# Mixer rounds 2, 3, 21, 22 and 23 reordered, and the memory panels of the stick-breaking half rounded one step later

## The chip, the cores and the metric

The kernel runs as one program on one core of a Trainium2 chip. The metric is the device time of one execution in microseconds (us). The kernel before took 2021.67 us (median of three runs, 2021.38 to 2026.02).

## The reference, cut to what matters

A sequence of 256 tokens of width 1024 (float32) goes through two blocks.

- First block, two layers. Each: `ada = silu(c) @ w_ada[l] + b_ada[l]` (1024 x 6144) gives shifts, scales and gates; `h = rms_norm(x) * (1 + sc) + sh`; `h @ w_in[l]` (1024 x 4888) gives the queries, keys and values of two mixers and the branch gates. The first mixer (NSA, 8 heads of width 64) attends three times: to 15 compressed blocks, to selected blocks (here all four, so causal attention) and to a window (causal too). The second mixer (MoBA) is causal attention over 8 heads. Their outputs go through `w_up_nsa`, `w_up_moba`, the gates and `w_out`, then a SwiGLU follows.
- Second block, two layers, each with two half SwiGLUs, a mixer and a cross attention to a memory of 256 tokens. The mixer of its layer 0 has a differential half and a stick-breaking half. The stick-breaking half is, for each of 8 heads, with z the scaled scores:

```
log_beta = log_sigmoid(z)
log_keep = where(strict, log_sigmoid(-z), 0)
later = cumsum(log_keep, reversed) - log_keep
w = where(strict, exp(log_beta + later), 0);  out = w @ v
```

The cross attention's keys and values are `rms_norm(mem) @ xm_w_kv` (1024 x 1024, in four panels of 512 rows by 512 columns).

## The kernel before, in words

**Weights.** All weights stream through `ring`, three slots of 1 MB, in the order of one list of panels (`weight_panels`). A panel holds 4 x 128 rows by 512 columns. SyncE issues a panel's DMA when the panel three places before it is released. Each dense product is made in three matmuls of rounded parts: high weight part x high and low activation part, and low weight part x high activation part. So each dense panel is split: ScalarE (ACT) copies it to the rounded high part ("hi", 2048 elements a partition, L753), VectorE (DVE) subtracts to get the low part ("lo", L2362) and releases the slot. The parts lie in two buffers, so a high part waits until TensorE (PE) has used the panel two before. `splits.until(key, ahead)` in an engine's program makes all parts in the list that are still to be made up to that panel and `ahead` more dense ones. Panels of `w_ada` are not multiplied on PE: VectorE multiplies and adds them itself, four passes over 512 columns for each half ("ada half", L2366 and L2371), and releases them. In the first block's mixers the list alternates: win4.0, win4.1, ada a, win5.0, ada b, win5.1, ada c, gbr0.0, and so on to gbr3.1, ada, nsa0 (`w_up_nsa`), ada, nsa1, moba0, moba1.

**Mixer rounds.** Each first-block layer has one loop of 27 rounds over 24 heads (8 selected, 8 window, 8 MoBA). Every engine has a loop of its own over i. PE in round i: scores of head i (L1758), transposes of the probabilities of head i-2 (L1770), weighted values of head i-3 (L1783), and two of the steps of the dense work beside it (a step is one chunk of 128 rows, 6 or 12 matmuls, L1550), which write banks from the pair `FILL`, freed by ScalarE's evacuation (two copies to `tok` and, for some, two squares to `sq`). VectorE in round i: the mask pass of head i (`masked`, L2590), which gives the row maxima `nmax`; then two steps of its side list (`more`), which hold the low parts. ScalarE: the copy of the transposed head i-2 (`turned_copy`), two exponentials of head i (`exps`, which wait for `nmax`), then its two steps of `more`, which hold high parts and evacuations. Engines run in order; between them there are only semaphores.

In round 3 VectorE adds mask and scale to the compressed scores (`cmp_s`, tile `feat`), takes the maximum and subtracts it ("cmp shifted"), and ScalarE exponentiates them ("cmp probs"). PE transposes the NSA output `y` at the end of round 21 (`tr y`, banks 6 and 7); ScalarE rounds it to the high part of `y_mix` (`y_copies`) in round 22, VectorE makes its low part (`y_lo`, which frees the two banks) in round 23. In round 23 PE opens banks 6 and 7 for the last four MoBA heads ahead of the weighted values of head 20. In round 24 PE starts `w_up_nsa`, which needs the low part of nsa0, `y_lo`, and banks 4 and 5, which VectorE frees in `moba_out(0)` in round 23.

**Stick half.** In `diff_mixer` the second loop has 11 rounds over 8 heads. PE in round i: z of head i, `later` of head i-1 (L2153 to L2155, waits for "keep"), weighted values of head i-3, two steps of the memory's keys and values (`kv_steps`, panels xkv0.0, xkv0.1, xkv1.0, xkv1.1; L1550). ScalarE: softplus of head i (Abs, Exp, Ln on `sq`), the exponential of head i-2, then two steps of `kv_beside(0)`, with high parts and evacuations (`kv_out`). VectorE: for head i three passes to "keep" (`rot`), one pass for head i-1 (`log weight`), one for head i-2 (`weight`), two steps of its own `kv_beside` (low parts, sums of squares, key normalization), and the entries of the dictionary `between`, which finish the differential half.

Of the kernel before, what the change touches and what calls it, by code (L numbers as in the profile page):

```python
# [112 lines left out]
class Tally:  # L113
# [19 lines left out]
    def at(self, key):  # L133
        if self.known is None:
            return self.sems("dve_step"), 1
        name, n = self.known[0][key]
        return self.sems(name), n
# [114 lines left out]
def build(nc, w, known):  # L252
# [7 lines left out]
    with ExitStack() as ctx:  # L260
# [490 lines left out]
        def _(act):  # L751
# [134 lines left out]
            def kv_beside(l):  # L886

                for g in range(2):
                    for n in range(2):
                        for k in range(4):  # L890
                            if k == 3:
                                if n:
                                    squared = kv_out(l, g)
                                splits.until(((("xkv", l), g, n)), 1 if g and n else 2)
                            if g == 1 and n == 0 and k == 2:
                                rsqrts(normed)
                            yield
                    if g == 0:
                        normed = squared

            def rsqrts(squared):

# [122 lines left out]
            def first_block(l):  # L1025
                norm(("mix", l), ("win", l), lambda c: adac[:, l, c:c + 1], ORDER[0])
                pieces = {0: [(0, 8, HD, "nq")], 1: [(C_KS - 512, 2, HD, "ks")],
                          2: [(0, 2, HD, "kw")], 3: [(0, 8, HD, "mq")]}

                def win_out(i):  # L1030
                    squared = []
                    for t in range(TT):
                        squared += evacuate((("win", l, i), t),
                                 [(0, EDGES[i + 1] - EDGES[i], tok_in[:, t, EDGES[i]:EDGES[i + 1]])],
                                 pieces[i])
                    return squared

                for i in ORDER[0:3]:
                    splits.until((("win", l), i, 1), 2)
                    rsqrts(win_out(i))  # L1040

                for kv in range(2):
                    job = ("hid", l, kv)
                    b = psum[:, tally.bank(job), 0:32].rearrange("p (g n) -> p g n", g=2)
                    act.wait_ge(*at(("full", job)))
                    act.wait_ge(*at(("pads", l)))
                    done = [("hid act", l, kv), ("free", job)]
                    if kv == 0:
                        run(hid_k[:, :, 0:NCMP], b[:, :, 0:NCMP], ACT.Gelu_apprx_tanh,
                            "act_hidden", *done)  # L1050
                    else:
                        for g in range(2):
                            run(hid_v[:, g, :, 0:NCMP], b[:, g, 0:NCMP].unsqueeze(1).broadcast_to(
                                [P, 4, NCMP]), ACT.Gelu_apprx_tanh, "act_hidden",
                                *(done if g else ()))
                splits.until((("win", l), 3, 0), 2)
                for j in range(2):
                    copies(("tr nq", l, j), nq_t[:, 2 * j:2 * j + 2, :])
                act.wait_ge(*at(("tok", (("win", l, 2), 1))))
                run(gates[:], tok_in[:, :, C_G:C_QB], ACT.Sigmoid, "act_gates", ("nsa gates", l))  # L1060
                act.preload_act_table_set(EXP_LN)
                copies_apart(("tr ks", l), gk_t[:, 0:1])
                squared = win_out(3)
                job = ("kc", l)
                k = n_sq[0]
                n_sq[0] += 1
                act.wait_ge(*at(("full", job)))
                act.wait_ge(*at(("sq read", k - 2)))
                b = psum[0:16, tally.bank(job), 0:2 * HD]
                run(kcn[:], b.rearrange("p (g d) -> p g d", g=2), ACT.Copy, "act_tok", ("tok", job))  # L1070
                run(sq[0:16, k % 2, 0:2 * HD], b, ACT.Square, "act_sq", ("sq", k), ("free", job))
                rsqrts(squared)
                act.wait_ge(*at(("sq read", k)))
                rsqrt(rs[0:16, k % 4, 0:2], ss[0:16, k % 4, 0:2], HD, "act_rs", ("rs", k))

                heads = mixer_heads(l)
                base = n_att[0]
                n_att[0] += HEADS
                more = beside(l)
                for i in range(HEADS + LAG + 1):  # L1080
                    if i == 15:
                        copies_apart(("tr mk", l, 0), mk_t[0])
                    if LAG <= i < HEADS + LAG:
                        m = i - LAG
                        turned_copy(heads[m], base + m)
                    if i < HEADS:
                        exps(heads[i], base + i,
                             heads[i]["n"] + (8 if heads[i]["st"][0] == "win" else 0))
                    if i == 0:
                        splits.until((("win", l), 3, 1), 2)  # L1090
                    if i == 1:
                        job = ("tr kc", l)
                        act.wait_ge(*at(("full", job)))
                        act.wait_ge(*at(("kc zeros", l)))
                        for g in range(2):
                            r = slice(HD * g, HD * g + HD)
                            run(kc_t[r, 16 * g:16 * g + 16], psum[r, tally.bank(job), 0:16], ACT.Copy,
                                "act_copied", *([("copied", job), ("free", job)] if g else []))
                        copies_apart(("tr kw", l), gk_t[:, 1:2])
                    if i == 3:  # L1100
                        act.wait_ge(*at(("cmp shifted", l)))
                        run(cmp_s, cmp_s, ACT.Exp, "act_step", ("cmp probs", l))
                    if i == 9:
                        for j in range(2):
                            copies(("tr mq", l, j), mq_t[:, 2 * j:2 * j + 2, :])
                    if i == 16:
                        act.wait_ge(*at(("full", ("scores", ("win", l), 7))))
                        copies_apart(("tr mk", l, 1), mk_t[1])
                    if i == 22:
                        for j in range(2):  # L1110
                            y_copies(("tr y", l, 0, j), 2 * j, y_mix)
                    if i == 25:
                        y_copies(("tr y", l, 1, 0), 4, y_mix)
                    for _ in range(UNITS):
                        next(more, None)
                    if i == 5:
                        copies(("cmp turn", l), cmp_pt)
                for _ in more:
                    pass
                y_copies(("tr y", l, 1, 1), 6, y_mix)  # L1120
                for g in range(2):
                    for i in range(2):
                        if g == 0:
                            splits.until((("w_up_moba", l), i, 0), 2)
                        c = 4 * g + 2 * i
                        act.wait_ge(*at(("merged sum", l, c)))
                        run(h[:, 0, c:c + 2, :], rot[:, i, :].rearrange("p (c s) -> p c s", s=S),
                            ACT.Copy, "act_hi", ("merged hi", l, c))
                splits.until((("wout", l), 1, 1))
# [1230 lines left out]
        def _(dve):  # L2360
# [360 lines left out]
            def first_block(l):  # L2721
# [160 lines left out]
                for i in range(HEADS + LAG + 1):  # L2882
                    if i < HEADS:
                        masked(heads[i]["st"], heads[i]["i"], con("causal"), HD ** -0.5)
                    if i - 1 in ADA_AT and pending:
                        ada_take(*pending.pop(0))
                    if i == 4:
                        splits.until(("ada", *ADA_GROUPS[st][0], 1))
                    if i == 5:
                        compressed_weights()  # L2890
                        ks_mk = [head_sums(8, HD) for t in range(TT)]
                        for _ in range(UNITS):
                            next(more, None)
                    if i == 22:
                        splits.until(("ada", *ADA_GROUPS[st][5], 0))
                    if i == 23:
                        for j in range(2):
                            y_lo(("tr y", l, 0, j), 2 * j, y_mix)
                    if i and i != 4:
                        for _ in range(UNITS):  # L2900
                            next(more, None)
                    if i == 0:
# [175 lines left out]
            def diff_mixer():  # L3078
# [103 lines left out]
                def difference_normed(t):  # L3182
# [10 lines left out]
                lb = shifted  # L3193
                more = kv_beside(0)
                between = {0: difference, 1: difference_sums,
                           3: lambda: difference_normed(0), 4: lambda: difference_normed(1)}
                for i in range(11):
                    if i < 8:
                        job = ("z", i)
# [397 lines left out]
```

## Time and profile before

| | |
|---|---|
| median of three runs | 2021.67 us |
| the profiled execution | 2020.08 us |
| its span | 2018.2 us |
| PE busy | 1971.9 us (98%) |
| VectorE busy | 1465.6 us (73%) |
| ScalarE busy | 1099.4 us (54%) |
| mean granted clock of TensorE | 0.997 |

The profile is of one execution; its span leaves out what lies before the first and after the last instruction. In a timeline row the first number is the start, the second how long the row's instructions took together, and the bracket, where there is one, is how long the engine was idle just before and what released it. Rounds are found by counting heads: the mixer loop of layer 0 runs from 87 to 220 us, that of layer 1 from 517 to 650 us, the stick half from 1162 to 1212 us.

### The profile page before, as it was taken

The page shows a single profiled execution, that of the slowest core. Times are in us where ns is not written, and L with a number is a line of the kernel's source. Part 1 is how long each engine was busy: PE and PEld are TensorE (multiplying, and loading weights), DVE is VectorE, ACT ScalarE, POOL GpSimd, SP SyncE. Part 2 cuts the span into 40 slices and gives each one's busy share as a digit, 9 for nine tenths or more (in the row PEclk, how much of TensorE's full clock was granted, in tenths as well). Part 3 has the DMA queues.
Part 4 walks back from the last instruction along what each step waited for, and adds up shares of the span by engine and source line. Part 5 has one row for each costly group of instructions (what it writes and reads, how often), then busy time and mean ns, then how long its engine had stood idle before and what let it go on. Part 6 is the DMA issues. An engine that isn't in the chain of part 4 may idle for free. (4 is left out here: it accounts for less than half of the span.)

```text
span 2018.2 us, 32166 instructions
## 1 busy us (share of the span) xinstructions
PE 1971.9 (98%) x12902; PEld 1772.6 (88%) x12902; DVE 1465.6 (73%) x2326; ACT 1099.4 (54%) x1744; POOL 30.1 (1%) x66
## 2 busy tenths in 40 slices
PE   8999999999999999999999989999999999999999
PEld 5889988898799988898898879888898899899888
DVE  7888788858797786567757586777667748767774
ACT  4655554534665455455546666655455537855552
POOL 1001000000010000000000000000000000000000
PEclk9999999999999999999999999999999999999999
DMA  9566568765566485556556334455555554235554
GB/s 352 164 208 210 188 206 265 264 204 169 169 215 218 150 271 182 184 178 188 188 169 206 127 104 147 147 188 186 175 183 188 188 178 128 94 126 168 188 178 136
DMA packets 266213, 372.24 MB, mean 184 GB/s; under 512 B 8400, under 2 KB 160336, under 8 KB 266064
## 3 DMA queue, kind: packets, MB, share of 16 engines
q1 hardware_dynamic: 264736, 368.91, 56.0%
q8 instruction: 103, 1.69, 0.3%
q10 hardware_dynamic: 1328, 1.26, 0.2%
q14 instruction: 46, 0.38, 0.1%
HBM read 369.09 MB, written 1.05 MB: 183 GB/s over the span
## 5 line engine op out<-in xcount | busy, mean ns | idle before, releaser
L2362 DVE TENSOR_TENSOR parts<-ring,parts 128x2048 fp32r<-128x2048 f32 (+2 forms) x304 | 675.9, 2223 | 398.8 <-ACT parts L753 398.4
L753 ACT ACTIVATE parts<-ring 128x2048 fp32r<-128x2048 f32 (+2 forms) x304 | 565.4, 1860 | 541.9 <-PE psum L1558 320.4
L1558 PE MATMUL psum<-h,parts 128*128 128x512 f32 x1920 | 679.0, 397 | 0.0
L1556 PE MATMUL psum<-h,parts 128*128 128x256 f32 x1920 | 541.8, 282 | 0.0
L1558 PEld LDWEIGHTS psum<-h,parts 128*128 128x128 f32 x1920 | 362.1, 189 | 87.5
L1556 PEld LDWEIGHTS psum<-h,parts 128*128 128x128 f32 x1920 | 360.6, 188 | 1.7 <-DVE parts L2362 1.4
L1550 PE MATMUL psum<-h,parts 128*128 128x256 f32 (+1 forms) x2088 | 257.3, 282 | 4.8 <-DVE h L2371 2.2
L1550 PEld LDWEIGHTS psum<-h,parts 128*128 128x128 f32 (+1 forms) x2088 | 245.8, 188 | 7.8 <-issue 3.3
L1550 PE MATMUL psum<-parts,h 128*128 128x512 f32 (+1 forms) x864 | 208.0, 392 | 8.1 <-ACT sq L753 3.6
L1550 PEld LDWEIGHTS psum<-parts,h 128*128 128x128 f32 x864 | 156.7, 191 | 41.2 <-issue 6.1
L1550 PE MATMUL psum<-hid_hl,parts 128*128 128x256 f32 x1584 | 190.9, 283 | 0.9 <-DVE parts L2362 0.9
L1550 PEld LDWEIGHTS psum<-hid_hl,parts 128*128 128x128 f32 x1584 | 189.5, 189 | 2.6 <-DVE parts L2362 2.5
L1558 PE MATMUL psum<-hid_hl,parts 128*128 128x512 f32 x528 | 185.6, 394 | 0.0
L1556 PE MATMUL psum<-hid_hl,parts 128*128 128x256 f32 x528 | 149.6, 283 | 0.2 <-DVE parts L2362 0.2
L753 ACT ACTIVATE tok<-psum 128x512 f32<-128x512 f32 (+3 forms) x156 | 90.0, 577 | 74.5 <-PE psum L1558 61.3
L1558 PEld LDWEIGHTS psum<-hid_hl,parts 128*128 128x128 f32 x528 | 99.3, 188 | 22.5
L1556 PEld LDWEIGHTS psum<-hid_hl,parts 128*128 128x128 f32 x528 | 99.4, 188 | 0.5 <-DVE parts L2362 0.5
L753 ACT ACTIVATE scores_area<-scores_area,nmax 128x256 f32<-128x256 f32 (+1 forms) x160 | 72.2, 455 | 50.6 <-DVE nmax L2590 50.3
L2362 DVE TENSOR_TENSOR tok<-psum,tok 128x512 f32<-128x512 f32 x120 | 82.1, 684 | 1.9 <-ACT tok L753 1.6
L753 ACT ACTIVATE scores_area<-psum 128x384 f32<-128x384 f32 (+1 forms) x80 | 39.7, 496 | 52.0 <-PE psum L1770 51.7
L2371 DVE SCALAR_TENSOR_TENSOR feat<-ring,scol,feat 128x512 f32<-128x512 f32 x84 | 63.4, 755 | 3.8
L2590 DVE CUSTOM_DVE_ANT_0 scores_area<-psum,const,sums 128x128 f32<-128x128 f32 (+1 forms) x96 | 37.3, 427 | 37.2 <-PE psum L1758 32.3
(271 smaller groups left out, 2128.5 us busy)
## 6 DMA issues: line engine op xcount, KB each, us to landing
ring<-in_w_ffn_in SPq DMA_DIRECT2D x88, 512.0 KB, 4.9
ring<-in_ffn_w_gate SPq DMA_DIRECT2D x88, 512.0 KB, 4.0
ring<-in_ffn_w_up SPq DMA_DIRECT2D x88, 512.0 KB, 5.0
ring<-in_w_ada SPq DMA_DIRECT2D x43, 1024.0 KB, 5.4
ring<-in_w_in SPq DMA_DIRECT2D x36, 1024.0 KB, 5.1
ring<-in_ffn_w_down SPq DMA_DIRECT2D x32, 1024.0 KB, 5.1
ring<-in_w_ffn_out SPq DMA_DIRECT2D x16, 1024.0 KB, 5.0
ring<-in_ffn_w_down SPq DMA_DIRECT2D x16, 768.0 KB, 4.4
```

Source lines behind the costliest of these rows:

```text
L753: act.activation(out, in_, func, **kw).then_inc(*sig(name, *keys))
L1550: mm = pe.matmul(out, left, right, start=start and n == 0, stop=stop and n == 2, skip_group_check=True)
L1556: pe.matmul(bank[:, 0:S], wt_hl[1], act[:, 0, :], start=start, stop=False, skip_group_check=True)
L1558: return pe.matmul(bank.rearrange("p (a s) -> p a s", a=2), wt_hl[0], act, start=False, stop=stop, skip_group_check=True)
L2362: dve.tensor_tensor(out, a, b, op).then_inc(*sig(name, *keys))
L2371: dve.scalar_tensor_tensor(out=out, in0=a, scalar=s, in1=b, op0=op0, op1=op1, **kw).then_inc(*sig(name, *keys))
L2590: dve.tensor_tensor_reduce(to, of, add, times, 3.0e38, ALU.add, ALU.min, nmax[:, n % 3, t:t + 1]).then_inc(*sig("dve_nmax", *keys))
```

## The change

ScalarE, mixer loop: the exponential of the compressed scores in round 3 goes behind the two steps of that round; the two `y_copies` go from round 22 to round 21. VectorE, mixer loop: round 2 makes only the ada half and leaves its two steps to round 3, behind the mask pass of head 3 and ahead of the compressed scores; the two `y_lo` go from round 23 to round 22, ahead of the ada half; the two steps of round 22 (low part of nsa0) go to round 23, behind the mask pass of head 23. Stick half, ScalarE: each high part that stood at the end of an odd round (k == 3) is made one step later, in the next even round, behind its softplus and exponential. Stick half, VectorE: `difference_normed(1)` goes from round 4 to round 5. No operation is added or taken out, and PE's program is unchanged.

```diff
@@ kv_beside(l), ScalarE
                         for k in range(4):
-                            if k == 3:
-                                if n:
-                                    squared = kv_out(l, g)
-                                splits.until(((("xkv", l), g, n)), 1 if g and n else 2)
+                            if k == 0 and (g or n):
+                                splits.until((("xkv", l), *((g, 0) if n else (0, 1))), 2)
+                            if n and k == 3:
+                                squared = kv_out(l, g)
                             if g == 1 and n == 0 and k == 2:
                                 rsqrts(normed)
                             yield
                     if g == 0:
                         normed = squared
+                splits.until((("xkv", l), 1, 1), 1)
@@ first_block(l), ScalarE
-                    if i == 3:
-                        act.wait_ge(*at(("cmp shifted", l)))
-                        run(cmp_s, cmp_s, ACT.Exp, "act_step", ("cmp probs", l))
...
-                    if i == 22:
+                    if i == 21:
                         for j in range(2):
                             y_copies(("tr y", l, 0, j), 2 * j, y_mix)
...
                     for _ in range(UNITS):
                         next(more, None)
+                    if i == 3:
+                        act.wait_ge(*at(("cmp shifted", l)))
+                        run(cmp_s, cmp_s, ACT.Exp, "act_step", ("cmp probs", l))
@@ first_block(l), VectorE
+                    if i == 2:
+                        splits.until(("ada", *ADA_GROUPS[st][0], 0))
+                    if i == 3:
+                        for _ in range(UNITS):
+                            next(more, None)
                     if i == 4:
                         splits.until(("ada", *ADA_GROUPS[st][0], 1))
...
                     if i == 22:
+                        for j in range(2):
+                            y_lo(("tr y", l, 0, j), 2 * j, y_mix)
                         splits.until(("ada", *ADA_GROUPS[st][5], 0))
                     if i == 23:
-                        for j in range(2):
-                            y_lo(("tr y", l, 0, j), 2 * j, y_mix)
-                    if i and i != 4:
+                        for _ in range(UNITS):
+                            next(more, None)
+                    if i and i not in (2, 4, 22):
                         for _ in range(UNITS):
                             next(more, None)
@@ diff_mixer(), VectorE
                 between = {0: difference, 1: difference_sums,
-                           3: lambda: difference_normed(0), 4: lambda: difference_normed(1)}
+                           3: lambda: difference_normed(0), 5: lambda: difference_normed(1)}
```

## Rows read from the trace of the kernel before

**Rows 1.** Page, part 1: busy time of each engine.
```profile
PE 1971.9 (98%) x12902; PEld 1772.6 (88%) x12902; DVE 1465.6 (73%) x2326; ACT 1099.4 (54%) x1744; POOL 30.1 (1%) x66
```
**Rows 2.** Waits of PE, whole span: us in total, times, longest.
```profile
...
PE psum L1783 <- DVE y_mix L2362: 4.1, 2, 2.1
PE psum L2153 <- DVE rot L2362: 4.0, 2, 2.6
PE psum L1550 <- ACT sq L753: 3.6, 2, 1.8
...
```
**Rows 3.** Timeline of PE, layer 0, rounds 3 and 4.
```profile
...
102.17 3.01 PE L1550 MATMUL psum<-parts,h 128*128 128x512 f32 x12
...
108.57 4.59 PE L1550 MATMUL psum<-parts,h 128*128 128x512 f32 x12 [1.79 <-ACT sq L753]
...
```
**Rows 4.** Windows: PE, PEld, DVE, ACT, POOL busy (x), PEclk, DMA share, GB/s.
```profile
...
109.00:112.60 3.60, 3.60 (x11) 2.79 (x10) 0.82 (x2) 2.51 (x6) 0.00 (x0) 0.53 0.45 114
...
203.00:207.00 4.00, 1.93 (x17) 1.77 (x16) 3.23 (x11) 0.99 (x4) 0.00 (x0) 1.00 1.03 392
...
```
**Rows 5.** Timeline of ACT, layer 0, round 3.
```profile
...
104.66 0.40 ACT L753 ACTIVATE scores_area<-scores_area,nmax 128x128 f32<-128x128 f32 x1 [2.38 <-DVE nmax L2590]
...
106.11 0.42 ACT L753 ACTIVATE feat<-feat 128x256 f32<-128x256 f32 x1 [0.46 <-DVE feat L2362]
106.43 0.58 ACT L753 ACTIVATE tok<-psum 128x512 f32<-128x512 f32 x1
...
```
**Rows 6.** Timeline of DVE, layer 0, rounds 2 and 5.
```profile
...
101.79 2.29 DVE L2362 TENSOR_TENSOR parts<-ring,parts 128x2048 fp32r<-128x2048 f32 x1
...
113.85 0.29 DVE L2590 CUSTOM_DVE_ANT_0 scores_area<-psum,const 128x128 f32<-128x128 f32 x1 [3.99 <-PE psum L1758]
...
```
**Rows 7.** Timeline of PE, layer 0, rounds 23 and 24.
```profile
...
205.33 0.85 PE L1783 MATMUL psum<-tok,scores_area 128*128 128x64 f32 x6 [2.07 <-DVE y_mix L2362]
...
208.41 3.08 PE L1550 MATMUL psum<-y_mix,parts 128*128 128x256 f32 x24
...
```
**Rows 8.** Timeline of ACT, layer 0, rounds 21, 22 and 26.
```profile
...
198.15 1.92 ACT L753 ACTIVATE parts<-ring 128x2048 fp32r<-128x2048 f32 x1 [1.05 <-DMA ring<-in_w_up_nsa]
...
201.21 1.06 ACT L753 ACTIVATE y_mix<-psum 128x512 fp32r<-128x512 f32 x2
...
217.69 1.92 ACT L753 ACTIVATE parts<-ring 128x2048 fp32r<-128x2048 f32 x1
...
```
**Rows 9.** Timeline of DVE, layer 0, round 23.
```profile
...
203.90 1.28 DVE L2362 TENSOR_TENSOR y_mix<-psum,y_mix 128x512 fp32r<-128x512 f32 x2
...
205.88 0.76 DVE L2362 TENSOR_TENSOR y<-psum,wt 128x256 f32<-128x256 f32 x2
...
```
**Rows 10.** Timeline of SyncE's queue: issues of the panels moba0 and moba1.
```profile
...
203.07 7.17 SPq L674 DMA_DIRECT2D ring<-in_w_up_moba  x2
...
```
**Rows 11.** Timeline of PE, stick half, round 6.
```profile
...
1196.30 0.67 PE L2153 MATMUL psum<-rot,const 128*128 128x256 f32 x2 [2.55 <-DVE rot L2362]
...
1197.84 4.60 PE L1550 MATMUL psum<-parts,mem_hl 128*128 128x512 f32 x12
...
```
**Rows 12.** Timeline of ACT, stick half: high part, then softplus of head 4.
```profile
...
1183.21 1.93 ACT L753 ACTIVATE parts<-ring 128x2048 fp32r<-128x2048 f32 x1
1185.01 0.50 ACT L753 ACTIVATE sq<-psum 128x384 f32<-128x384 f32 x1
...
```
**Rows 13.** Timeline of DVE, stick half: heads 4, 5, 7, and log weight 7.
```profile
...
1186.66 0.56 DVE L2371 SCALAR_TENSOR_TENSOR scores_area<-psum,sq 128x384 f32<-128x384 f32 x1 [2.48 <-ACT sq L753]
...
1194.41 0.56 DVE L2371 SCALAR_TENSOR_TENSOR scores_area<-psum,sq 128x384 f32<-128x384 f32 x1
...
1204.75 0.56 DVE L2371 SCALAR_TENSOR_TENSOR scores_area<-psum,sq 128x384 f32<-128x384 f32 x1 [1.44 <-ACT sq L753]
...
1208.61 0.55 DVE L2362 TENSOR_TENSOR scores_area<-scores_area,psum 128x384 f32<-128x384 f32 x1
...
```
**Rows 14.** Timeline of PE: first output product behind the stick half.
```profile
...
1213.73 2.97 PE L1550 MATMUL psum<-y_ab,parts 128*128 128x256 f32 x24 [1.03 <-ACT y L753]
...
```

## The prediction

> **What bounds the kernel now.** I read the page's busy shares first: PE is busy for 1971.9 us of a span of 2018.2 [rows 1]. Its work is unchanged, so the change can only pay through the 46.3 us in which PE is idle, and through the clock at which its matmuls run. The next view is PE's list of waits. Three of its entries lie where the change works: 3.6 us in two waits for ScalarE's `sq`, 4.1 us in two waits for VectorE's `y_mix`, 4.0 us in two waits for VectorE's `rot` [rows 2]. PE's timeline places them: round 4 of each first mixer, round 23 of each, and rounds 5 and 6 of the stick half. That is 11.7 us of waiting. Last I read the granted clock around them. Behind the round 4 wait the same 12 matmuls that take 3.01 us a round earlier take 4.59 [rows 3], and the window there has a mean clock of 0.53 [rows 4]: TensorE is at 1.2 instead of 2.4 GHz. The 12 matmuls behind the stick half's 2.55 us wait show it again with 4.60 us [rows 11]. Behind the 2.07 us wait of round 23 the clock is 1.00 [rows 4]. So three of the six waits touch or precede a fall, at 1.6 us each, 4.7 us in all (I take layer 1's round 4 as layer 0's: rows 2 has both waits as one entry with nearly equal parts). A perfect change would bring 11.7 + 4.7 = 16.4 us.
>
> **Round 4 (twice).** PE needs two banks whose contents ScalarE must first copy and square. Today VectorE does the ada half and the 2.29 us low part in round 2, and only then the mask pass of head 3; ScalarE idles 2.38 us for it and starts the exponentials at 104.66, then waits until 106.11 for the compressed scores, and starts the four evacuating passes at 106.43 [rows 5]. They last until PE is released at 108.57 [rows 3], 2.14 us with the hand-over. In the new order the mask pass takes the place of the low part, which began at 101.79 [rows 6], so the exponentials start about 2.2 us earlier, at 102.5, and end (they took 106.11 - 0.46 - 104.66 = 0.99 us) at 103.5. The exponential of `cmp_s` no longer stands ahead, so the evacuation waits only for the products of round 3. Those are the 12 matmuls of 102.17 to 105.18 [rows 3]; the first token tile is complete three matmuls before the end (3 x 0.25 us), at 104.4 to 104.6. The four passes then hand over at 104.5 + 2.14 = 106.6 to 106.7. PE asks at 108.57 - 1.79 = 106.78. The wait goes, by a margin of only 0.1 us; I take 1.75 us of it.
> What is late next: the low part now ends at about 104.7, and PE asks for it at 106.78; the compressed scores are subtracted at 106.1, as today. The exponential of `cmp_s` slips behind the next high part, to about 109, and its reader on VectorE comes behind the mask pass of round 5, where VectorE idles 3.99 us for PE today [rows 6]. That idle time also lets VectorE follow PE when PE comes 3.3 us earlier.
> With the wait goes the slow stretch: 4.59 - 3.01 = 1.58 us. Bounds for this term: 0 (the fall comes all the same) to 1.6. I take 1.58, since the equal matmuls without a wait all took 3.01. Per mixer 1.75 + 1.58 = 3.33, twice: 6.7 us.
>
> The Trainium skill ("TensorE: Matmul & The Clock Gate", HAM oscillation) warns of idle gaps well longer than the 1.79 us seen here; by it this gap alone would not bring a fall, and the sum would lose the clock terms, 4.7 us. The rows disagree, so I keep them. The same page says that where the clock moves differs from run to run; that is what the second rival below would look like.
>
> **Round 23 (twice).** PE waits for banks 6 and 7, which the `y_lo` passes free; these run at 203.90 to 205.18 [rows 9], and PE goes on at 205.33 [rows 7]. New order: ScalarE idles 1.05 us for a DMA before the high part of nsa0 at 198.15 [rows 8], so the two `y_copies` (1.06 us) fit into this idle time, at 197.1 to 198.2, and delay nothing. VectorE makes `y_lo` (1.28 us) from about 198.0 to 199.3, 4 us before PE's need at 205.33 - 2.07 = 203.26. The 2.07 us wait goes.
> What is late next: in round 24 PE wants the low part of nsa0 and banks 4 and 5 at 208.41 - 2.07 = 206.34 [rows 7]. VectorE's work to there keeps its length, since the passes only change places: mask pass, `y_lo`, ada half, mask pass 23, low part, `moba_out(0)`, which today ends at 205.88 + 0.76 = 206.64 [rows 9]. It had no large wait for others in this stretch, so it ends at 206.3 to 206.7 again: 0 to 0.4 us of new waiting. The low part is ready about 1.1 us ahead. I take 1.87 us of gain per mixer, 3.7 in all; bounds 1.5 and 2.07 each.
> DMAs: the slot of nsa0 is released some 2.2 us later, so moba0 is issued at about 205.3 instead of 203.07 [rows 10]. Its high part is wanted at 217.69 - 2 [rows 8], 10 us later. nsa1's panel is issued 1.3 us later; its high part too lies several us behind. No cost.
>
> **Stick half.** Today the softplus of head 4 starts at 1185.01 behind a high part that began at 1183.21 [rows 12]: 1.80 us. VectorE idles 2.48 us for it and starts head 4 at 1186.66; from there to its log weight 7 at 1208.61 is 21.95 us, of which it idles 1.44 [rows 13]. That stretch is the same work whatever its order: 20.5 us. Without the high part ahead, head 4 starts at 1186.66 - 1.80 = 1184.86. The 1.44 us idle (head 7's softplus waits for z of head 7, which PE gives after its 2.55 us wait and the slow matmuls) vanishes too, since PE reaches that point some 5 us earlier and VectorE only some 3. So log weight 7 comes at 1184.86 + 20.51 = 1205.37, 3.24 us earlier. Behind it stand ScalarE's last exponential, `y_copies`, a high part and the copy of `y` that releases PE at 1213.73 [rows 14], all of which shift with it.
> PE would save 4.0 of waiting and 1.6 of slow clock here, 5.6 us; but VectorE's chain ends the half, so 2.4 us come back as waits for "keep" of heads 5 and 7 and for the last weights. Moving `difference_normed(1)` behind head 5 shortens PE's wait in round 6 and leaves the chain's length as it is: 0. The first high part (xkv1.0) is made one step later too, about when VectorE asks for it; as VectorE waits 2.48 us before head 4 anyway, a miss of some tenths is hidden there. I take 3.2 us; bounds 1.8 (only the softplus comes earlier) and 4.5.
>
> **Sum.** 6.7 + 3.7 + 3.2 = 13.6 us. Against the profiled execution's 2020.08 us that is 2006.5 (span 2004.6). The median of the runs lies 1.6 us above that execution: 2008.1 us, 0.67% faster. About 0.3% (6 us) is what a measurement of this kernel can tell from no change.
>
> **Rivals.**
> (a) The clock's falls come back, moved: short waits of about 1 us remain in the stick half, and other stretches shift. For it: 2.07 us waits without a fall and 1.79 us waits with one, so a wait alone doesn't decide. Against: the slow matmuls found in these loops all stand behind waits that go. Three falls at 1.58: 2008.1 + 4.7 = 2012.8. Chance 0.13.
> (b) Round 4's margin of 0.1 us fails: the evacuation starts late (first tile complete only near 105.2, or the exponentials late), the wait keeps 0.5 us or more and the fall stays in one or both mixers. Then up to 6.7 us less: 2011 to 2014.8. Chance 0.13.
> (c) The change doesn't do what it says for the sum: VectorE can't follow PE in the mixers; PE then waits for mask passes and returns all of round 4's gain and some of the rest: 2016 to 2020, within 0.3%. For it: VectorE is the busiest engine beside PE [rows 1]. Against: VectorE idles 3.99 us for PE in round 5 [rows 6], so it is ahead there. Chance 0.08.
> (d) Slower: the queue behind `y_lo` in round 22. VectorE now waits there for ScalarE's `y_copies`, and ScalarE for PE's transposes of round 21; ada half, mask pass 23, low part of nsa0 and `moba_out(0)` all stand behind it, and PE's round 24 behind them. Each us beyond the 0.4 counted is paid twice (two mixers). It decides from a `y_lo` that ends 7 us late, at about 206: 2 x 7 = 14 us would eat the sum, 9 us late gives 2026. Against: `y_copies` finds room in ScalarE's 1.05 us of idle time, and the transposes it waits for are a round old by the time VectorE asks. Chance 0.04.
> The forecast itself has 0.62 (2004.5 to 2011).
>
> **How the numbers follow.** Forecast 2008.1. The range takes in (a), (b) and the lower bounds of the terms: 2004.5 to 2015.5; about 0.86 of the cases lie in it, and the rest I leave for what isn't listed. Faster by over 0.3% (below 2015.6): 0.62 + 0.13 + 0.13 = 0.88, of which I give 0.03 to the middle: 0.85. Same 0.10, slower 0.05.
>
> **What would show it.** Right: PE's waits for `sq` in round 4 and for `y_mix` in round 23 are gone or under 0.5 us; every group of 12 matmuls in the loops takes 3.0 us; the softplus of head 4 stands directly behind the evacuation; log weight 7 comes 20 to 21 us after head 4's first pass; PE waits up to 1 us for "keep" of head 7. Wrong: a wait for `nmax` or for a low part in rounds 5 to 8 or 24; a fall of the clock at another place; VectorE idle in front of `y_lo` in round 22.

## The result, and the profile after

| | before | changed |
|---|---|---|
| median | 2021.67 us | 2010.10 us (5 runs, 2007.13 to 2010.92) |
| the profiled execution | 2020.08 us | 2010.10 us |
| its span | 2018.2 us | 2008.2 us |
| mean granted clock of TensorE there | 0.997 | 0.999 |

The ratio of changed to before is 0.9935, with a 95% interval of 0.9923 to 0.9947: 13 us faster (11 to 16). The medians lie 11.6 us apart.

PE's list of waits in the changed kernel is the first thing to read against [rows 2]. (Columns: engine, tile and line, the releaser, us in total, times, longest. The changed file has one line more above PE's code, so L1550 is L1551 here, and so on.)

```profile
...
PE psum L1551 <- DVE parts L2363: 7.2, 16, 1.2
PE psum L1551 <- DVE h L2372: 4.7, 7, 1.4
PE psum L2154 <- DVE rot L2363: 1.9, 2, 1.1
...
PE psum L1759 <- ACT y L753: 1.5, 1, 1.5
...
PE psum L1551 <- DVE y L2363: 0.7, 2, 0.5
...
```

The entries for `sq` and `y_mix` are gone. `rot` went from 4.0 to 1.9 us. New is a wait of 0.7 us in two parts for VectorE's `y`, the banks that `moba_out` frees.

PE's timeline of the changed kernel, layer 0, rounds 3 and 4 and then round 24, answers to [rows 3] and [rows 7]:

```profile
...
103.23 3.00 PE L1551 MATMUL psum<-parts,h 128*128 128x512 f32 x12
...
107.75 2.99 PE L1551 MATMUL psum<-parts,h 128*128 128x512 f32 x12
110.58 0.82 PE L1759 MATMUL psum<-y,feat 128*128 128x128 f32 x4
...
204.44 2.98 PE L1551 MATMUL psum<-y_mix,parts 128*128 128x256 f32 x24 [0.48 <-DVE y L2363]
...
```

The matmuls of round 4 start without a wait and take 2.99 in place of 4.59 us. ScalarE's timeline (against [rows 5]) shows how near this was:

```profile
...
103.51 0.40 ACT L753 ACTIVATE scores_area<-scores_area,nmax 128x128 f32<-128x128 f32 x1 [0.18 <-DVE nmax L2591]
...
105.58 0.60 ACT L753 ACTIVATE tok<-psum 128x512 f32<-128x512 f32 x1 [1.08 <-PE psum L1551]
...
107.03 0.62 ACT L753 ACTIVATE sq<-psum 128x512 f32<-128x512 f32 x1
108.01 1.92 ACT L753 ACTIVATE parts<-ring 128x2048 fp32r<-128x2048 f32 x1 [0.36 <-DMA ring<-in_w_in]
109.83 0.40 ACT L753 ACTIVATE feat<-feat 128x256 f32<-128x256 f32 x1
...
```

The wait for `nmax` fell from 2.38 to 0.18 us, the evacuation now waits 1.08 us for PE's own products, and its last square ends at 107.65, 0.1 us before PE uses the banks. The exponential of the compressed scores (109.83) runs behind the high part and nobody waits for it.

In the stick half, VectorE's and PE's timelines of the changed kernel (against [rows 13] and [rows 14]):

```profile
...
1178.16 0.56 DVE L2372 SCALAR_TENSOR_TENSOR scores_area<-psum,sq 128x384 f32<-128x384 f32 x1 [0.70 <-ACT sq L753]
...
1194.90 0.56 DVE L2372 SCALAR_TENSOR_TENSOR scores_area<-psum,sq 128x384 f32<-128x384 f32 x1
...
1198.75 0.55 DVE L2363 TENSOR_TENSOR scores_area<-scores_area,psum 128x384 f32<-128x384 f32 x1
...
```

```profile
...
1186.20 0.67 PE L2154 MATMUL psum<-rot,const 128*128 128x256 f32 x2 [0.82 <-DVE rot L2363]
...
1196.78 0.67 PE L2154 MATMUL psum<-rot,const 128*128 128x256 f32 x2 [1.08 <-DVE rot L2363]
...
1203.88 2.30 PE L1551 MATMUL psum<-y_ab,parts 128*128 128x256 f32 x18 [1.03 <-ACT y L753]
...
```

From head 4's first pass to log weight 7 it is 1198.75 - 1178.16 = 20.59 us, without the 1.44 us of idle time of before: the 20.5 us of the forecast. PE's waits for "keep" of heads 5 and 7 are 0.82 and 1.08 us.

One thing is new. The clock fell at another place, in front of the differential half's heads, where PE waits 1.48 us for ScalarE's `y`. The wait itself is old: the trace of before has the same 1.48 us there (at 1113.02), with full speed behind it. PE's timeline and the window of the changed kernel (columns as in [rows 4]):

```profile
...
1104.72 0.89 PE L1759 MATMUL psum<-y,feat 128*128 128x128 f32 x4 [1.48 <-ACT y L753]
1106.01 4.59 PE L1551 MATMUL psum<-parts,h 128*128 128x512 f32 x12 [0.40 <-ACT tok L753]
...
```

```profile
...
1106.00:1110.00 4.00, 3.99 (x11) 3.18 (x12) 2.67 (x6) 2.98 (x6) 0.00 (x0) 0.60 0.49 192
...
```

Both traces hold the same 12902 matmuls in the same order, so the shift of one and the same matmul's start gives the account:

| stretch | shift it adds (us) |
|---|---|
| before the first matmul (7.83 -> 8.86) | +1.03 |
| layer 0, round 4 (112.44 -> 110.11) | -3.36 |
| layer 0, rounds 23 and 24 (208.41 -> 204.44) | -1.64 |
| small, up to layer 1's mixer | -0.27 |
| layer 1, round 4 (542.75 -> 535.01) | -3.50 |
| layer 1, rounds 23 and 24 (638.40 -> 628.75) | -1.91 |
| SwiGLU of layer 1, a wait of 0.72 us for a low part (723.83 -> 715.04) | +0.86 |
| small, up to the differential half | +0.50 |
| differential half, the new fall of the clock | +1.57 |
| stick half (1209.67 -> 1199.82) | -3.13 |
| to the end | -0.18 |
| sum | -10.03 |

### The profile page after: what moved, and what is told of

It reads as the page before. It is cut to its first block and busy times, and to the rows that moved or that the text cites. A ratio compares the mean times of both kernels' runs of the same rounds, so it can differ in the third digit from the quotient of the medians.

```text
span 2008.2 us, 32166 instructions
## 1 busy us (share of the span) xinstructions
PE 1967.7 (98%) x12902; PEld 1768.3 (88%) x12902; DVE 1465.9 (73%) x2326; ACT 1100.1 (55%) x1744; POOL 30.1 (1%) x66
## 5 line engine op out<-in xcount | busy, mean ns | idle before, releaser
L1551 PE MATMUL psum<-h,parts 128*128 128x256 f32 (+1 forms) x2088 | 256.7, 281 | 5.2 <-DVE h L2372 2.4
L1551 PEld LDWEIGHTS psum<-h,parts 128*128 128x128 f32 (+1 forms) x2088 | 245.3, 187 | 8.2 <-issue 3.4
L1551 PE MATMUL psum<-parts,h 128*128 128x512 f32 (+1 forms) x864 | 206.3, 390 | 4.6 <-DVE h L2372 2.3
L1551 PE MATMUL psum<-hid_hl,parts 128*128 128x256 f32 x1584 | 190.9, 283 | 0.9 <-DVE parts L2363 0.9
L1551 PEld LDWEIGHTS psum<-hid_hl,parts 128*128 128x128 f32 x1584 | 189.5, 189 | 2.6 <-DVE parts L2363 2.5
L1551 PEld LDWEIGHTS psum<-parts,h 128*128 128x128 f32 x864 | 155.3, 190 | 37.2 <-issue 6.2
```

The costliest lines, as they stand in the source:

```text
L1551: mm = pe.matmul(out, left, right, start=start and n == 0, stop=stop and n == 2, skip_group_check=True)
```

## The experiments

All were compared with the kernel before on the same chip; that kernel was executed 53 times beside them, and each execution comes with its mean granted clock. "A fall" is a stretch in which the granted clock is 0.5, that is 1.2 in place of 2.4 GHz.

**e1, rounds 2 and 3 alone** (the edits of ScalarE's round 3 and VectorE's rounds 2 and 3 of the diff above, nothing else).

> The kernel before with the edits of rounds 2 and 3 alone. Theory (PE's wait in round 4 and the 1.2 GHz stretch behind it are one cause): the 1.8 us wait goes in both mixers and the 12 matmuls behind it take 3.0 us in place of 4.6; 6.5 to 7 us faster than before, all of it gained between the start and the end of round 4 of each mixer, the 2.07 us waits of round 23 stay. Rival (the falls of the clock have their own timing): only the waits go, 3.6 us faster, and some 12 matmuls elsewhere take 4.6 us.

Measured: 2018.88 against 2021.54 us, ratio 0.9982 (0.9973 to 0.9992): 3.6 us faster, 2 to 5. In the profiled execution the shift between round 3 and round 5 is -3.5 us in each mixer, as the theory has it. But the unchanged 2.07 us wait of round 23 now had a fall behind it, where before it had none. PE's wait and the window behind it in e1:

```profile
...
203.06 0.91 PE L1783 MATMUL psum<-tok,scores_area 128*128 128x64 f32 x6 [2.07 <-DVE y_mix L2362]
...
```

```profile
...
204.00:207.00 3.00, 3.00 (x15) 3.00 (x15) 2.79 (x6) 0.00 (x0) 0.00 (x0) 0.50 0.59 216
...
```

So the rival is right for the times (3.6 us, what the waits alone are worth; the 6.5 to 7 us of the theory are out) and the theory for this one trace's round 4.

**e2, rounds 21 to 23 alone** (`y_copies` in round 21, `y_lo` in round 22, the low part of nsa0 in round 23).

> The kernel before with the edits of rounds 21 to 23 alone. Theory: PE's 2.07 us wait in round 23 goes and 0.2 to 0.5 us of it come back in round 24 as a wait for moba_out: 3.2 to 3.7 us faster; the waits and the slow matmuls of round 4 stay. Rival (what is gained there is lost again by the end of the mixer, as VectorE can't follow): within 1 us of before.

Measured: 2017.44 us, ratio 0.9973 (0.9962 to 0.9985), 5.5 us faster, 3 to 8. PE's waits of 2.07 and 2.08 us became 0.48 and 0.19 us, 3.5 us by the trace. The 5.5 us of the times are more than the 3.2 to 3.7 us expected, which the interval still takes in. The first row here is what matters for the clock: the untouched 1.79 us wait of layer 0's round 4, and this time full speed behind it. (The equal wait of layer 1, 1.83 us, has a fall behind it in this trace too.)

```profile
...
108.61 3.00 PE L1550 MATMUL psum<-parts,h 128*128 128x512 f32 x12 [1.79 <-ACT sq L753]
...
205.29 2.98 PE L1550 MATMUL psum<-y_mix,parts 128*128 128x256 f32 x24 [0.48 <-DVE y L2362]
...
```

**e3, the stick half alone** (`kv_beside` and `difference_normed(1)` in round 5).

> The kernel before with the edits of the stick half alone. Theory (VectorE's chain from head 4 to log weight 7 ends this half, and the edit starts it one high part, 1.8 us, earlier and takes its 1.4 us wait for head 7's softplus away): the first output product starts 3.2 us earlier, although PE's waits for rot and its slow stretch shrink by some 4 us; 3.2 us faster. Rival (PE's own waits set the pace): 5.6 us faster.

Measured: 2019.43 us, ratio 0.9990 (0.9980 to 1.0000), 2 us faster, 0 to 4. Its profiled execution had a span of 2023.7 us, longer than before, with five falls in the loops: at both round 4 waits, at both round 23 waits (in layer 0 it lasted twice as long as the others), and in front of the differential heads. Two of the windows:

```profile
...
110.00:114.00 4.00, 4.00 (x13) 3.09 (x12) 0.81 (x2) 2.50 (x6) 0.00 (x0) 0.57 0.50 142
206.00:210.00 4.00, 3.67 (x17) 3.71 (x18) 3.32 (x7) 0.00 (x0) 0.00 (x0) 0.51 0.76 288
...
```

The stick half itself is as in the changed kernel: from head 4's first pass (1193.09) to the first output product (1218.81) 25.72 us, against 25.72 there and 27.07 before. The trace of before had a fall inside this half, and those of e2 and e5 had none there: within the half each of the two gained 1.35 us on the trace of before without any edit in it. VectorE's first pass for head 7 shows where (before: 1.44 us of idle time in [rows 13]). First e2, then e7, whose trace has a fall in this half:

```profile
...
1202.52 0.56 DVE L2371 SCALAR_TENSOR_TENSOR scores_area<-psum,sq 128x384 f32<-128x384 f32 x1
...
```

```profile
...
1193.41 0.56 DVE L2372 SCALAR_TENSOR_TENSOR scores_area<-psum,sq 128x384 f32<-128x384 f32 x1 [1.48 <-ACT sq L753]
...
```

All five traces with a fall in the stick half (before, e1, e4, e6, e7) have this idle time, 1.43 to 1.48 us; e2 and e5, with the same 2.55 us wait of PE but no fall, have none. So the edit is worth 3.15 us against a half with a fall, and 1.8 us against one without. The measured 2 us (interval 0 to 4) is the average over executions; the 5.6 us of the rival are out.

**e4, `y_lo` early, `y_copies` late** (VectorE's side of e2; ScalarE unchanged). The diff is against e2:

```diff
-                    if i == 21:
+                    if i == 22:
                         for j in range(2):
                             y_copies(("tr y", l, 0, j), 2 * j, y_mix)
```

> The kernel before with VectorE's side of the edits of rounds 22 and 23, but ScalarE's y_copies left in round 22. Theory (rival d of the prediction has a real mechanism, and the move of y_copies is what keeps it out): VectorE idles some 4 us in front of y_lo in round 22, y_lo ends near 203.5 of the old time base, so PE's wait in round 23 shrinks to 0.3 us, but the ada half, the mask pass, the low part and moba_out are late and PE waits 4 us in round 24: 2.5 us slower per mixer, 5 us in all, up to 8 if the clock falls behind it. If VectorE has room to spare there: 3 to 4 us faster as with the full edit.

Measured: 2028.93 us, ratio 1.0038 (1.0027 to 1.0050): 7.7 us slower. VectorE's and PE's timelines:

```profile
...
201.27 1.29 DVE L2362 TENSOR_TENSOR y_mix<-psum,y_mix 128x512 fp32r<-128x512 f32 x2 [3.85 <-ACT y_mix L753]
...
206.40 2.29 DVE L2362 TENSOR_TENSOR parts<-ring,parts 128x2048 fp32r<-128x2048 f32 x1
...
209.38 0.76 DVE L2362 TENSOR_TENSOR y<-psum,wt 128x256 f32<-128x256 f32 x2
...
```

```profile
...
206.54 0.55 PE L1770 MATMUL psum<-const,scores_area 128*128 128x128 f32 x3 [1.51 <-DVE nmax L2590]
210.24 4.60 PE L1550 MATMUL psum<-y_mix,parts 128*128 128x256 f32 x24 [2.54 <-DVE y L2362]
...
```

VectorE idles 3.85 us, and all that stands behind it is late: PE waits 1.51 us for `nmax` and 2.54 us for `moba_out`, with a fall behind. The queue of rival (d) is real; since e4 differs from e2 in nothing else, the move of `y_copies` by one round is what keeps it out.

**e5 and e6, the two halves of the round 3 edit.** e5 moves only ScalarE's exponential, e6 only VectorE's mask pass.

> The kernel before with ScalarE's half of the round 3 edit alone (the exponential of the compressed scores behind the steps). Theory: the evacuation then starts right behind the exponentials of head 3, at about 105.7 in place of 106.4, so PE's wait in round 4 shrinks from 1.8 to about 1.0 us: 0.8 us per mixer, 1.6 us in all, plus up to 3.2 us if the falls of the clock go with it. Rival: this half alone does it all, 6.8 us faster.

> The kernel before with VectorE's half of the round 3 edit alone (mask pass of head 3 ahead of the low part). Theory: ScalarE's exponentials come 2.2 us earlier, but the exponential of the compressed scores still stands ahead of the evacuation and waits until about 106.1, so the evacuation starts at 106.4 as before: no change of PE's wait, 0 +- 1 us. Rival: the exponentials of head 3 were what mattered, and this half alone takes the wait: 3.6 to 6.8 us faster.

Measured: e5 2019.60 us, ratio 0.9991 (0.9981 to 1.0000); e6 2021.93 us, ratio 1.0002 (0.9992 to 1.0011), both against 2021.31. PE's wait in round 4, first e5, then e6 with ScalarE's timeline:

```profile
...
108.73 2.99 PE L1550 MATMUL psum<-parts,h 128*128 128x512 f32 x12 [0.92 <-ACT sq L753]
...
```

```profile
...
108.96 3.00 PE L1550 MATMUL psum<-parts,h 128*128 128x512 f32 x12 [1.78 <-ACT sq L753]
...
```

```profile
...
102.85 0.40 ACT L753 ACTIVATE scores_area<-scores_area,nmax 128x128 f32<-128x128 f32 x1 [0.18 <-DVE nmax L2590]
...
106.50 0.42 ACT L753 ACTIVATE feat<-feat 128x256 f32<-128x256 f32 x1 [2.65 <-DVE feat L2362]
106.82 0.58 ACT L753 ACTIVATE tok<-psum 128x512 f32<-128x512 f32 x1
...
```

Both as the theory had it. In e6 the mask pass comes early and ScalarE only waits longer in the next place, 2.65 in place of 0.46 us. The whole gain needs both.

**e7, `difference_normed(1)` back in round 4.**

```diff
-                           3: lambda: difference_normed(0), 5: lambda: difference_normed(1)}
+                           3: lambda: difference_normed(0), 4: lambda: difference_normed(1)}
```

> The changed kernel with difference_normed(1) back in round 4 of the stick half. Theory (it is 1.5 us of VectorE's chain wherever it stands between head 4 and head 7): log weight 7 and the first output product start at the same distance from head 4 as in the changed kernel, while PE's wait for keep of head 5 grows from 0.8 to 2.3 us and that for head 7 shrinks: same time within 0.5 us, or 1.6 us slower if the longer wait brings a fall of the clock that PE can't hide. Rival (the move is what gains): about 1.5 us slower with the output product 1.5 us later.

Measured: 2010.70 us, ratio to before 0.9945 (0.9928 to 0.9962); the times can't tell it from the changed kernel. The trace can: PE's wait for "keep" of head 5 is 2.42 us, a fall follows, z of head 7 is late, and VectorE idles 1.48 us for head 7's softplus (the row is shown under e3):

```profile
...
1184.91 0.95 PE L2154 MATMUL psum<-rot,const 128*128 128x256 f32 x2 [2.42 <-DVE rot L2363]
1202.40 2.97 PE L1551 MATMUL psum<-y_ab,parts 128*128 128x256 f32 x24 [1.03 <-ACT y L753]
...
```

From head 4 (1175.28) to the output product it is 27.12 us, 1.4 more than in the changed kernel, where an equal distance was expected. The 1.4 us are the idle time that came with the fall. That the move helps by shortening the wait, so that a fall is rarer there, is argued and not shown: it rests on this one trace and on a mean clock of 0.9983 in four executions, against 0.9992 in nine of the changed kernel.

**e8, low part of `w_out`'s first panel behind.** VectorE's 2.28 us pass leaves the chain between heads 6 and 7.

```diff
-                                splits.until((("xkv", l), g, n), 1 if l == 0 and g and n else 2)
+                                splits.until((("xkv", l), g, n), (0 if n else 1) if l == 0 and g else 2)
...
                     if i == 9:
+                        splits.until((("wout", 2), 0, 0))
                         for j in range(2):
```

> The changed kernel with one more edit: VectorE makes the low part of the first panel of w_out (2.28 us) behind weight 7, in round 9 of the stick half, in place of round 6. Theory (VectorE's chain ends the half): log weight 7 comes 2.2 us earlier, PE's 1.1 us wait for keep of head 7 goes, and the first output product starts 1.5 to 2.1 us earlier, bounded then by y_lo and ScalarE's copy: about 1.8 us faster than the changed kernel, 13.4 against before. Rival (the low part then is itself late, or the later release of its slot delays a panel): no gain or 1 us slower.

Measured: 2007.59 us, ratio to before 0.9928 (0.9914 to 0.9943). From head 4 (1177.66) to the output product (1201.56) 23.90 in place of 25.72 us: 1.8 us, as expected. The times don't show it: the changed kernel, executed again as e9, took 2007.41 us (0.9931 of before).

**e9, the changed kernel again; e10, 20 idle matmuls in front of the differential heads; e11, `moba_out(0)` first; e12, all three with e8** (e10 to e12 contain e8).

```diff
-                warm_in(ATT, 6)
+                warm_in(ATT, 20)
...
                     if i == 23:
+                        moba_out(0, base + 19)
                         for _ in range(UNITS):
                             next(more, None)
...
-                    if i == 23:
-                        moba_out(0, base + 19)
```

> The changed kernel once more, for its spread and its mean clock. Theory (a fall of the clock is brought on, in some executions and not in others, by a wait of PE of about 1.5 us or more, and the change takes away five of the six largest): the mean granted clock over its executions is 0.9993 to 0.9997, against 0.9974 over 43 executions of the kernel before, and its times spread over less than 5 us, where before spread over 8. Rival (the falls keep their number and only move): a mean clock of 0.997 to 0.998.

> The kernel with the low part of w_out behind, and 20 in place of 6 idle matmuls in front of the first scores of the differential half, where PE waits 1.48 us for ScalarE (1.5 us of filling, no other work). Theory (falls follow idle time of PE): the fall seen there in both the changed kernel and the one with w_out behind is gone, the mean clock is 0.9998 or more, and the median 0.5 to 1.2 us below that of the kernel with w_out behind. Rival (idle matmuls don't keep the clock, or they delay the scores): same or up to 0.5 us slower.

> The kernel with the low part of w_out behind, and moba_out(0) ahead of the low part of nsa0 in round 23. Theory: PE's waits of 0.48 and 0.19 us for the banks in round 24 turn into waits of 0 to 0.3 us for the low part: 0 to 0.6 us faster, which the times can't tell. Rival: the low part is late by its 1.4 us: 1 us slower per mixer.

> Low part of w_out behind, 20 idle matmuls, moba_out(0) first. If each holds: median 2006 to 2007, 14.5 to 15.5 us faster than the kernel before, mean clock 0.9998 or more.

| | median us | ratio to before | 95% interval | mean clock |
|---|---|---|---|---|
| before | 2020.65 (7) | | | 0.9973 (53 executions) |
| e9 | 2007.41 | 0.9931 | 0.9916 to 0.9946 | 0.9990 (4) |
| e10 | 2005.70 | 0.9923 | 0.9908 to 0.9938 | 1.0000 (4) |
| e11 | 2005.59 | 0.9922 | 0.9907 to 0.9936 | 1.0000 (4) |
| e12 | 2004.50 | 0.9918 | 0.9901 to 0.9934 | 1.0000 (4) |

e9: the changed kernel's nine executions have a mean clock of 0.9992 (a little below what was expected) against 0.9973, so the falls became rarer and didn't merely move. The other half of the theory, that it takes a wait of about 1.5 us, did not hold: the one fall in e9's trace stands behind 0.64 us (its rows are in the last section). e10: PE's 1.48 us wait is filled (20 idle matmuls for 2.35 us in place of 6 for 0.82) and its four executions have a mean clock of 1.000 each; but so have e11's, which has no extra idle matmuls, so e10 doesn't show that the filling did it. e11: the wait for `y` in round 24 became one for the low part:

```profile
...
203.44 2.98 PE L1551 MATMUL psum<-y_mix,parts 128*128 128x256 f32 x24 [0.42 <-DVE parts L2363]
...
```

0.42 in place of 0.48 us, and 0.28 in place of 0.19 us in layer 1: no gain, as expected. e12 is the fastest kernel of all, 2004.50 us where 2006 to 2007 were expected, 0.8% below before and 2.9 us below the changed kernel on the same chip. Its four executions all lie below e9's four, though the intervals of the two ratios overlap; which of its three edits brings how much can't be told.

## Why the prediction was right

The forecast was 2008.1 us, 13.6 us faster; measured were 2010.1 us, and 13 us (11 to 16) by the ratio.

- **Round 4.** Forecast 3.33 us per mixer, measured 3.36 and 3.50 in the pair of traces. The margin of 0.1 us was there, and it held; rival (b) didn't happen. e5 and e6 show that both halves of the working (mask pass, compressed scores) were needed. The 1.58 us of clock in each 3.33 are another matter, see below.
- **Round 23.** Forecast 1.87 us per mixer with 0 to 0.4 us of new waiting in round 24; measured 1.64 and 1.91, with 0.48 and 0.19 us of waiting for `moba_out`. The later DMAs cost nothing. Rival (d) has its price from e4, 7.7 us, but needs `y_copies` to be late.
- **Stick half.** Forecast 3.2 us, measured 3.13 in the traces. That VectorE's chain ends the half is right: it is 20.6 us long, and with a 2.3 us pass taken out of it (e8) the half is 1.8 us shorter by the trace. But the working explained the 1.44 us of idle time in it by PE's 2.55 us wait as well as by the slow matmuls, and took them as always there. e2 and e5 keep that wait, had no fall, and have no such idle time. e7, with the high parts moved and a fall as before, gained 1.76 us in the half. So 1.8 us of the 3.2 are the moved high part, and the rest is the clock. The move of `difference_normed(1)` was put at 0; e7's one trace, without the move, has a fall and 1.4 us more, and no trace has that kernel without a fall, so the 0 stays untested.
- **The clock, the term that was mis-sized.** The sum took the three falls of one trace as the kernel's own: 2 x 1.58 us in round 4 and about 1.4 us in the stick half, 4.6 us, all to be gained. Rival (a) was right in part. The same 1.79 us wait of layer 0 has a fall behind it in the traces of before and e3 and none in e2, e4 and e6; the 2.07 us wait of round 23 in layer 0 has none in before and e6 and one in e1, e3 and e5. By a straight line through 53 executions of the kernel before, 0.001 of mean clock goes with 1.8 us. So, as an estimate, its 0.0027 below 1 cost it 4.8 us a run, and the changed kernel's 0.0008 cost 1.4 us. 3.4 us of the change's gain are clock, on average, and about 10 us waits: mean times over all executions are 2021.96 and 2008.57 us.
- **Luck in the total.** Taken one by one, the parts didn't bring what the sum gave them: 3.6 us in e1 for the 6.7 of round 4, 5.5 in e2 for 3.7, and 2 in e3 for 3.2. The first forecast lies outside its measured interval of 2 to 5 us. The ratios multiply to 0.9982 x 0.9973 x 0.9990 = 0.9945, near the whole change's 0.9935. That the total came out within 1 us owes something to misses that cancel. The ten executions of e1 have a mean clock of 0.9977 and those of e2 0.9981, against 0.9973 before. That points at clock gained with the waits of round 23, to which the forecast gave none, but the two means are too near each other to show it.
- **The difference of the two traces** is 10.0 us and not 13.6, by +1.03 us before the first matmul, where nothing was changed, by +1.57 us for the fall in front of the differential heads, and by +0.86 us in a SwiGLU, where PE waited 0.72 us for a low part. That last wait isn't the change's own: e9, the same kernel, has none there, and e2 has 0.67 us at the same place. What brings it stays open, and so does the first term.

The Trainium skill ("TensorE: Matmul & The Clock Gate", HAM oscillation) warns of idle gaps longer than any of these waits. The traces disagree: falls stood behind waits of 0.61 to 2.55 us. The same page remarks that the clock's rise at a kernel's start comes earlier or later from run to run. The traces show something like it for the fall: before and e2 differ at one and the same wait of 1.79 us.

## What to carry to other kernels

On an engine that is 98% busy, list its few waits, find for each which other engine's queue is late, and put the pass that is waited for ahead of one that nobody waits for; two engines often have to be reordered together, and either half alone gives little (e5, e6) or does harm (e4). Follow the chain past the wait that is removed: in the stick half 4 us of waiting and a slow stretch were worth 2 to 3 us, since VectorE ended the half. And take the parts one by one: a total can come out right by parts that don't. A fall of the clock seen in one trace is a chance and not a property of the place: count it from the mean clock of many executions.

## What the runs showed of the hardware that was not expected

A fall of TensorE to 1.2 GHz cost about 1.6 us where PE had work all through (12 matmuls of 512 columns in 4.6 in place of 3.0 us) and came behind quite short waits. Three traces have one at the start of layer 1, behind 0.61 us (e4), 0.64 us (e9) and 0.66 us (e2), each after a stretch of small matmuls of 30 and 280 columns; the other traces have the same wait, 0.56 to 0.66 us, without a fall. PE's timeline of e9:

```profile
...
498.34 0.97 PE L1822 MATMUL psum<-feat,aux 128*128 128x30 f32 x8
499.95 4.35 PE L1551 MATMUL psum<-parts,h 128*128 128x512 f32 x11 [0.64 <-DVE parts L2363]
...
```

Falls explain much of the spread of the kernel before (2018.6 to 2027.6 us): its four executions with a mean clock of 0.995 took 2026.6 to 2027.6 us, the two with 0.999 took 2019.7 and 2020.2 us. It does not explain all: 22 executions with 0.997 took 2019.0 to 2024.5 us.
